# A feed-forward down projection as seven products of quarters

## What is computed

```python
up = rmsnorm(x, g_ffn_pre) @ ffn_w_up
ext = jnp.concatenate([conv_hist, up], axis=1)
c = ffn_conv_b
for j in range(CONV_W):
    c = c + ext[:, j: j + T] * ffn_conv_w[j]
act = jax.nn.gelu(c[..., :D_FF], approximate=True) * c[..., D_FF:]
x = x + rmsnorm(act @ ffn_w_down, g_ffn_post)
```

## Time and profile before

| | us |
|---|---|
| median of 3 runs (lowest to highest) | 1567.13 (1565.37 to 1569.6) |
| the profiled execution, its own time | 1567.42 |
| its span, first to last instruction | 1565.7 |
| TensorE busy | 1524.1 (97%) |
| VectorE busy | 898.4 (57%) |
| ScalarE busy | 583.8 (37%) |
| GpSimd busy | 300.0 (19%) |
| mean granted clock | 0.982 |

### The profile page before, as it was taken

The page is one execution under the profiler, slowest core; times in us unless marked ns, Lnnn a source line. Parts: engine busy times, 40 slices in busy tenths (PEclk is TensorE's granted clock), DMA queues, the critical chain, the costliest instruction groups (busy, mean ns, idle before and its releaser), DMA issues.

```text
span 1565.7 us, 26850 instructions
## 1 busy us (share of the span) xinstructions
PE 1524.1 (97%) x10067; PEld 1415.8 (90%) x10067; DVE 898.4 (57%) x1545; ACT 583.8 (37%) x1084; POOL 300.0 (19%) x293
## 2 busy tenths in 40 slices
PE   7999999999999999999997999999999999999997
PEld 7889999989999999997877999999999998788875
DVE  6575465657332233226558777777777775554644
ACT  7233132333222122114445444444444444453432
POOL 1124133340100000000124333333333320000000
PEclk9999999999999899999998999999999999999999
DMA  7234455451332432304114666655662138665471
GB/s 259 59 109 132 142 174 173 141 173 35 112 113 69 121 110 67 121 14 135 71 45 125 218 218 199 219 191 188 220 221 83 64 111 300 226 216 177 157 243 66
DMA packets 145809, 227.65 MB, mean 145 GB/s; under 512 B 14011, under 2 KB 116441, under 8 KB 144831
## 3 DMA queue, kind: packets, MB, share of 16 engines
q1 hardware_dynamic: 136711, 203.97, 40.8%
q0 software_dynamic: 8736, 22.08, 3.8%
q10 hardware_dynamic: 288, 0.59, 0.1%
HBM read 196.46 MB, written 74.34 MB: 173 GB/s over the span
## 4 chain that ended last, share of the span: by engine, by line
PE 91%; DVE 4%; DMA 2%; ACT 1%; issue 1%; SPq 0%; ACTq 0%; DVEq 0%
PE PS L1323 28%; PE PS L1144 19%; PE PS L1389 13%; PE PS L1039 9%; PE PS L1282 6%; PE PS L1020 4%; PE PS L1208 2%; PE PS L1096 2%; PE PS L1068 1%; PE PS L1384 1%; PE PS L1082 1%; PE PS L1252 1%; PE PS L1001 1%; DMA as_stage<-acts 1%; PE PS L1052 1%
## 5 line engine op out<-in xcount | busy, mean ns | idle before, releaser
L1323 PE MATMUL PS<-h_lo,wr_hi 128*128 128x264 f32 x1056 | 216.7, 286 | 0.0
L1323 PEld LDWEIGHTS PS<-h_lo,wr_hi 128*128 128x128 f32 x1056 | 165.6, 190 | 0.0
L1323 PE MATMUL PS<-t_hi,wr_hi 128*128 128x264 f32 x704 | 149.9, 292 | 7.6 <-DVE h_lo L2296 4.1
L2334 DVE TENSOR_TENSOR wd_lo<-wd_stage,wd_hi 128x1024 fp32r<-128x1024 f32 x66 | 80.8, 1224 | 118.3 <-ACT as_hi L1762 118.2
L1323 PE MATMUL PS<-h_hi,wr_hi 128*128 128x264 f32 x704 | 145.5, 288 | 0.7 <-DVE cext L2362 0.5
L1323 PE MATMUL PS<-t_hi,wr_lo 128*128 128x264 f32 x704 | 145.3, 286 | 0.0
L2020 DVE TENSOR_TENSOR tw_lo<-tw_stage,tw_hi 128x1024 fp32r<-128x1024 f32 (+1 forms) x28 | 32.6, 1166 | 177.7 <-ACT tw_hi L1533 177.5
L1323 PEld LDWEIGHTS PS<-t_hi,wr_hi 128*128 128x128 f32 x704 | 110.8, 191 | 9.1 <-DVE h_lo L2296 4.7
L1761 ACT ACTIVATE wd_hi<-wd_stage 128x1024 fp32r<-128x1024 f32 x66 | 69.8, 1057 | 130.9 <-PE PS L1389 76.6
L1144 PE MATMUL PS<-hT_hi,tw_hi 128*128 128x352 f32 x480 | 111.2, 342 | 1.8 <-issue 1.8
L1323 PEld LDWEIGHTS PS<-h_hi,wr_hi 128*128 128x128 f32 x704 | 108.9, 189 | 3.5 <-DVE wr_lo L2286 0.7
(11 more groups left out here) (317 smaller groups left out, 3444.3 us busy)
## 6 DMA issues: line engine op xcount, KB each, us to landing
wd_stage<-in_ffn_w_down SPq DMA_DIRECT2D x66, 512.0 KB, 3.6
tw_stage<-in_ffn_w_up SPq DMA_DIRECT2D x88, 256.0 KB, 4.8
out_k_s<-in_cache_k_w SPq DMA_DIRECT2D x8, 2044.0 KB
out_v_s<-in_cache_v_w SPq DMA_DIRECT2D x8, 2044.0 KB
qb<-zs SPq DMA_DIRECT2D x24, 512.0 KB, 5.1
acts<-cact POOLq DMA_DIRECT2D x22, 528.0 KB, 9.4
tw_stage<-in_w_in SPq DMA_DIRECT2D x20, 512.0 KB, 5.3
as_stage<-acts SPq DMA_DIRECT2D x44, 192.0 KB, 3.9
```

Of the source, the lines that this page charges most:

```text
L1323: last = pe.matmul(PS[:, bank + b, 0:BH], w[slot][:, k, :], x[:, k, b * BH:(b + 1) * BH], start=(k == 0 and j == 0), stop=(k == HK - 1 and ...
L2334: dve.tensor_tensor(wd_lo[slot][:, :], wd_stage[slot][:, :], wd_hi[slot][:, :].bitcast(F32), ALU.subtract)
```

## The change

The prompt rows of the down projection are cut in two halves of rows, the depth in two halves of 11 blocks, the columns in two halves of 512, and the product of the 2 x 2 quarters is made from seven products in place of eight. A product `n` has 11 steps `(n, k)`, each with 4 row tiles x 3 matmuls of 512 columns; its four tiles lie in four of six PSUM banks, one bank a tile. The three matmuls of a tile are consecutive.

The weights are loaded once in products 1 and 2 and kept (`dw`, 22 blocks of 1024 columns). One quarter of the activations is kept too (`dS`). The other quarters are loaded when needed into four staging buffers (`ds`). GpSimd makes the sums of quarters that Strassen's method needs, 110 operations of 128x512 named in `SUMS` (T1, T4a, T2, T3, T4b on weights; S1, S2, S3, Sa, Sb on activations), each waiting for the one before; they overwrite kept or staged data. Every step is split anew by ScalarE and VectorE, two copies and two subtractions of 128x512, into a ring of three buffers (`ring`); the last four steps of product 3 have buffers of their own. VectorE evicts the products and adds them into two arrays `C1` and `C2` (`evict`), ScalarE copies product 1.

The sample rows (`smp_d`) run apart, against the weights as they are split: the first 512 columns beside products 1 and 2 in bank 6, the second 512 columns as extra steps `(0, k)` in bank 7, each with a split of its own, between the steps of products 6 and 7.

The finishing (squares, gain, reciprocal, multiply and add, store) of the sample tile and of tiles 4 to 6 now lies among the steps of product 3, with the multiplication by the gain on GpSimd for three tiles (`scale_rows`); rows of x come in two buffers (`xrow`), the load of each after the store of the tile two before. Tile 7 and tiles 0 to 3 follow. The split of the fourth step stands behind the copy of the turned tails in ScalarE's order, and on SP the loads from `(1, 6)` on stand behind the wait for the stored convolution states.

The diff, cut to what the text speaks of (the lines taken away are the functions shown above):

```diff
--- before.py
+++ after.py
...
+        HK2, LATE = FC // 2, 4
+        PRODUCTS = (1, 2, 6, 7, 4, 5, 3)
+        SLOTS = []
+        for n in PRODUCTS:
+            for k in range(HK2):
+                SLOTS.append((n, k))
+                if n == 6 and k % 2 and k < 10:
+                    SLOTS.append((0, k // 2))
+                if n == 7 and k % 2 == 0:
+                    SLOTS.append((0, 5 + k // 2))
...
+        SUMS = [("T1", k) for k in range(HK2)] + [(c, k) for k in range(HK2) for c in ("S1", "T4a")]
+        SUMS += [(c, k) for k in range(HK2) for c in ("S2", "T2")] + [(c, k) for k in range(HK2) for c in ("S3", "T3")]
+        SUMS += [("T4b", k) for k in range(HK2)] + [("Sa", k) for k in range(HK2)] + [("Sb", k) for k in range(HK2)]
...
+            def load_down(x):
+                n, k = x
+                u = STAGE[x]
+                st, signal = ds[u % 4], wd_in[u % 4]
+                if u >= 4:
+                    m, l = STAGED[u - 4]
+                    sp.wait_ge(wd_lo_done, AT[STAGED[u - 4]] + 1)
+                    if m in (2, 3, 5):
+                        sp.wait_ge(d_sum, summed_at({2: "S1", 3: "Sb", 5: "Sa"}[m], l))
+                f = k + (HK2 if n in (2, 4, 3) else 0)
...
+            load_down((1, 4))
+            load_s(0)
+            load_down((1, 5))
+            sp.wait_ge(cnat_out, 32 * FC)
+            load_down((1, 6))
+            load_s(1)
+            load_down((1, 7))
+            sp.wait_ge(c_out, 7 * FC + U0)
+            load_s(2)
+            for i in range(2):
+                sp.wait_ge(act_out[i], 16 * (FC // 2))
+            load_smp(1)
+            load_down((1, 8))
...
+            def load_row(i):
+                n = FINAL[i]
+                t0, rows = tile_of(n)
+                if i >= 2:
+                    sp.wait_ge(y_ready, i - 1)
+                else:
+                    sp.wait_ge(wd_lo_done, AT[5, 1 + i] + 1)
+                sp.dma_start(xrow[i % 2][0:rows, :], x2s[t0:t0 + rows, :]).then_inc(wq_in[1][i % 2], 16)
...
+            for x in STAGED[9:]:
+                load_down(x)
+                if x == (3, 5):
+                    load_row(0)
+                    load_row(1)
+            for i in range(NTILE):
+                store_y(i)
+                if i + 2 < NTILE:
+                    load_row(i + 2)
 
...
+            def down_sum(c, k, out, a, b, op):
+                if SUMS.index((c, k)):
+                    pool.wait_ge(d_sum, summed_at(c, k) - 1)
+                pool.tensor_tensor(out, a, b, op).then_inc(d_sum, 1)
...
+            for k in range(HK2):
+                pool.wait_ge(wd_lo_done, AT[1, k] + 1)
+                down_sum("T1", k, dw[k][:, low], dw[k][:, high], dw[k][:, low], ALU.subtract)
+            for k in range(HK2):
+                st = staged(2, k)
+                pool.wait_ge(x_in[k // 4], 16 * (4 if k < 4 else 3))
+                down_sum("S1", k, dS[:, k, :], dS[:, k, :], st[:, 1, :], ALU.add)
+                pool.wait_ge(wd_lo_done, AT[2, k] + 1)
+                down_sum("T4a", k, dw[HK2 + k][:, low], dw[HK2 + k][:, low], dw[k][:, low], ALU.add)
+            for k in range(HK2):
+                st = staged(6, k)
+                down_sum("S2", k, st[:, 0, :], dS[:, k, :], st[:, 0, :], ALU.subtract)
+                down_sum("T2", k, st[:, 1, :], dw[HK2 + k][:, high], dw[k][:, low], ALU.subtract)
+            for k in range(HK2):
+                st = staged(7, k)
+                down_sum("S3", k, st[:, 0, :], st[:, 0, :], st[:, 1, :], ALU.subtract)
+                down_sum("T3", k, st[:, 1, :], dw[HK2 + k][:, high], dw[k][:, high], ALU.subtract)
+            for k in range(HK2):
+                down_sum("T4b", k, dw[HK2 + k][:, low], dw[HK2 + k][:, high], dw[HK2 + k][:, low], ALU.subtract)
+            for k in range(HK2):
+                st = staged(5, k)
+                pool.wait_ge(wd_lo_done, AT[5, k] + 1)
+                down_sum("Sa", k, dS[:, k, :], dS[:, k, :], st[:, 0, :], ALU.subtract)
+
+            def scale_rows(i):
+
+                rows = finished(FINAL[i])
+                pool.wait_ge(o_ss, 9 + i + 1)
+                pool.tensor_tensor(rows, rows, in_halves(gfin[:, :]), ALU.mult).then_inc(t_sums, 1)
+            for k in range(HK2):
+                st = staged(3, k)
+                down_sum("Sb", k, dS[:, k, :], st[:, 0, :], dS[:, k, :], ALU.subtract)
+                if k == 6:
+                    pool.wait_ge(gain_in, 64)
+                    scale_rows(1)
+                elif k == 8:
+                    scale_rows(2)
+            scale_rows(3)
...
+            def tile_part(x, i):
+                n, k = x
+                r, bank = ring(x), (4 * PRODUCTS.index(n) + i) % 6
+                for j, (a, w) in enumerate(((da_hi, dw_hi), (da_hi, dw_lo), (da_lo, dw_hi))):
+                    mm = pe.matmul(PS[:, bank, :], a[r][:, i * P:(i + 1) * P], w[r][:, :],
+                                   start=(k == 0 and j == 0), stop=(k == HK2 - 1 and j == 2))
+                return mm
...
+                if n == 1 and k == 2:
+                    turn_tails(FC - 1)
+            for i in range(4):
+                for x in SLOTS[-LATE:]:
+                    pe.wait_ge(wd_lo_done, AT[x] + 1)
+                    mm = tile_part(x, i)
+                    if i == 3:
+                        mm.then_inc(wd_used, 1)
+                if i < 3:
+                    mm.then_inc(f_mm, 1)
...
+            def split_down(x):
+                n, k = x
+                r = ring(x)
+                if n in (1, 2, 4):
+                    act.wait_ge(wd_in[STAGE[x] % 4], stage_in[x])
+                for c in {4: ("T4b",), 5: ("S1", "T1"), 7: ("T3",), 6: ("T2",), 3: ("Sb",)}.get(n, ()):
+                    act.wait_ge(d_sum, summed_at(c, k))
...
+                    act.wait_ge(p_done, 7 * FC - 3 + U0)
+                if r >= 3:
+                    act.wait_ge(wd_lo_done, AT[5, HK2 - 1] + 1)
+                elif AT[x] >= 3:
+                    act.wait_ge(wd_used, AT[x] - 2)
+                w, a = operands(x)
+                act.activation(dw_hi[r][:, :], w, ACT.Copy)
+                act.activation(da_hi[r][:, :], a, ACT.Copy).then_inc(wd_hi_done, 1)
...
+            for s_, x in enumerate(SLOTS[3:], 3):
+                split_down(x)
...
+                if x == (2, 1):
+                    act.wait_ge(act_out[1], 16 * (FC // 2))
+                    act.wait_ge(wd_used, AT[1, HK2 - 1] + 1)
+                    for i in range(4):
+                        act.activation(C1[:, i, 512:D], PS[:, i, :], ACT.Copy).then_inc(u_out, 1)
+                if x[0] == 3 and 3 <= x[1] < 8:
+                    square(x[1] - 3)
...
+            def evict(n, i):
...
+                p = PRODUCTS.index(n)
+                bank = PS[:, (4 * p + i) % 6, :]
+                left, right = C1[:, i, 0:512], C1[:, i, 512:D]
+                if i < 3:
+                    dve.wait_ge(f_mm, 3 * (p - 1) + i + 1)
+                else:
+                    dve.wait_ge(wd_used, AT[n, HK2 - 1] + 1)
+                if FREED.index((n, i)):
+                    dve.wait_ge(f_free, FREED.index((n, i)))
...
+            dve.wait_ge(cnat_done, FC)
+            for x in SLOTS[3:]:
+                low_down(x)
+                n, k = x
...
+                    if n == 4:
...
+                    for i in range(4):
+                        evict(PRODUCTS[PRODUCTS.index(n) - 1], i)
+                if x == (4, 7):
+                    fold()
+                if n == 3 and k >= 5 and k < 9:
+                    finish(k - 5)
...
```

More of the change, by code:

```diff
@@ L818, in _ @@
-            for n in range(6, NTILE):
-                store_y(n)
+                dst = ys if n == 8 else yp[n * P:n * P + P]
+                sp.dma_start(in_halves(dst), finished(n)).then_inc(y_out[i % 3], 16)
+            for x in STAGED[9:]:
[7 more added lines that the diff above has]
+                    load_row(i + 2)
@@ new lines, in tile_part, with sample_part @@
+            def tile_part(x, i):
[5 more added lines that the diff above has]
+                return mm
+            def sample_part(bank, f, w_hi_, w_lo_, first, last):
+                passes = ((2 * TS, w_hi_), (TS, w_lo_))
+                for j, (both, w) in enumerate(passes[::-1] if last else passes):
+                    mm = pe.matmul(PS[0:both, bank, :], smp_d[f // HK2][:, f % HK2, 0:both], w[:, :],
+                                   start=(first and j == 0), stop=(last and j == 1))
+                return mm
@@ L1852, in _ @@
+            for i in range(5, NTILE):
+                square(i)
         @block.vector
@@ new lines, in fold, with scale_rows @@
+            def fold():
+                dve.wait_ge(wd_lo_done, AT[4, 5] + 1)
+                both = PS[0:2 * TS, 6:8, :]
+                dve.tensor_copy(finished(8), both[TS:2 * TS, :, :]).then_inc(t_step, 1)
+                dve.wait_ge(t_step, U0 + 11)
```

(28 more changed lines are left out.)

346 lines of the change are left out of this document (180 added, 166 removed).

## The result

The changed kernel takes 1608.15 us (median of 4 runs, 1603.6 to 1613.9), the kernel before beside it 1567.4: a ratio of 1.0262, 95% interval 1.0226 to 1.0297. The forecast was 1585 with a range up to 1603: the side was right, the size (+17.6) less than half of the +41 that came. The profiled execution has 1608.4 around a span of 1606.7, 41.0 more than before.

What follows compares the result with a forecast made beforehand. The prediction took TensorE's matmuls to bound the down projection. Terms -30.0 - 1.1 + 3.4 + 4 + 4.9 + 20 + 1.5 + 14 + 0.9 = +17.6 on 1567.4 gave 1585 us, range 1559 to 1603.

Steps and rivals of the forecast that it cites:

- Matmuls: Down projection: full-row matmuls fall from 1056 to 924, 132 fewer at 0.227 us each, -30.0 us.
- the one bank: Three matmuls in a row add into one PSUM bank where two alternate before; forecast at no price.
- the gap after the tails: Sign in product 1: a TensorE gap of about 3 us after the convolution tails are turned.
- The port: Products 6 and 7: GpSimd sums and VectorE subtractions take turns; at least +14, +26.6 by step count, +20 us taken.
- Product 3: Evictions, finishes, GpSimd's wide product and a row load delay the last four steps; +19.5 by step count, +14 us taken.
- Product 1: Start of product 1: fourth step's split waits behind gelu and tails copy, +3.4 us; late loads for steps 7 and 8, +4.
- The heap on SP: Product 1: 5.7 MB of loads come together after the stored convolution states, 13.7 us at 416 GB/s; +4 us, bounds 0 and 6.
- Wait ahead of (6,0): After product 2, GpSimd's late sums delay the first split of product 6: +4.9 us (3.5 to 6.5).
- Head of product 4: Evictions of product 7 stand behind the split of (4,1): +1.5 us (0 to 2.5).
- Tail: Behind the last matmul, an eviction then two finishes take 6.8 us where it was 5.9: +0.9 us.
- -1.1: Down projection before the change: TensorE's one gap of 1.11 us falls away with the 4.2 MB load of x.
- The rival with the clock: TensorE's idle time in products 6, 7 and 3 lowers the granted clock; 1600 us or a little more, chance 0.13.

Runs made afterwards that it cites:

- the first experiment: Changed kernel, with subtractions from split (6,2) to the end of product 7 taking PSUM as second operand: 1587.95 us, ratio 1.0126 to the kernel before.

## Why the prediction fell short, point by point

**Matmuls.** Right: steps of 2.72 and 3.19 wherever nothing is late (product 2 is dense for 35.10), so no price for the one bank. Of the signs that were named, the gap after the tails (about 3, measured 2.90) came; sums of 1.51 (1.7), a TensorE busy for 81% of products 6 and 7 (75 to 80) and 9.1 us of gaps ahead of the last four steps (10 or more) came nearly.

**The port.** The mechanism was right, shown by the first experiment; the size was not. I had followed it step by step with strict turns to +26.6, had a floor of +14, and took the middle, +20. Measured: +30.8. Taking the middle is the step that failed. The rows behind it had turns in them wherever the two kinds of operation met and no case of their missing each other, so nothing spoke for the half towards the floor. The floor itself left out the sums for product 4, which run in this stretch: GpSimd made 51 sums there (x51 in the table beside the added matmuls) and VectorE 66 subtractions, two for each of 33 steps. By an estimate from the earlier trace rows that is 51 x 1.28 + 66 x 0.45 = 95 us of one port; counted in the two timelines, one or the other engine was at such an operation for 95.8 of the 101.0. The rest is in places that I had costed apart or at nothing: an eviction stands behind a split that is late itself (4.58 at the head of product 7).

**Product 3.** The step count said +19.5 (its terms add up to 19.2), I took +14 as between it and 0; measured 49.2 - 29.9 = +19.3. The same error. The count had the cause right: wide products on GpSimd, finishes in front of splits, a late row of x (one finish waited 4.29). That it fits to the tenth is luck: by an estimate 1.9 us of the 19.3 are the slow matmuls behind the last wait, which it didn't have.

**Product 1.** +3.4 and +4 forecast, +11.0 measured. The wait ahead of (1,3) came as 2.90. For it I had named two things in front of the split, the gelu and the copy behind it; the copy is worth 0.3, the gelu and VectorE's product are the wait. The gelu began 10.1 us after the first matmul, 1.2 sooner than before and not 2.5. The heap on SP was there, but two parts of the step were wrong. From 1312.70 to 1328.00 DMA moved 337 GB/s, not 416; and I had not seen the split of the sample rows, which waits for its place in the heap ahead of (1,7). So (1,7) began 9.2 us late, where the forecast had 7.4 for the whole product. The other 1.7 are the four steps behind it at the lower clock, which stood at nothing.

**The rest.** Wait ahead of (6,0): +4.9 forecast, 5.04 measured. Head of product 4: +1.5, measured 1.8. Tail: +0.9, measured 1.8. At nothing stood a wait of 1.10 ahead of (3,0), by which the stretch of product 5 is 1.3 too long, and a start of the stage that is 1.65 later. With -30.0 and -1.1 the measured terms give -31.1 + 1.65 + 11.0 + 5.0 + 30.8 + 1.8 + 1.3 + 19.3 + 1.8 = +41.5, against a span that grew by 41.0.

**The rival with the clock.** It had 1600 or a little more, and the time came out there, with a clock that fell as it said (0.89 in product 6). Still it is not the main reason: in products 6 and 7 the length stayed with the clock brought back. Its price shows only in the lengths of products 1 and 3, behind their last waits: 1.6 us, and by the estimate above 1.9. A time that fits a rival doesn't prove its mechanism. The range ended at 1603 because I gave that case only its beginning; with both step counts in place of the middles the sum would have been 1585 + 6.6 + 5.5 = 1597.

**Open.** 25.4 of the 30.8 us in products 6 and 7 go with their sums and seven of those for product 4; how much the seven hold, and how the other 5 divide between evictions and splits, wasn't taken apart. Nor was the load of the sample rows from the rest of the heap, nor the price of the lower clock in product 3.

## What to carry to other kernels

Before work is put on an idle engine, look whether it shares a path with the engine that feeds the bound one: here GpSimd's sums and VectorE's subtractions of two SBUF tiles make one queue, and their times add up: in strict turns a sum and a subtraction took about 1.7 together. Giving most of both to VectorE, in an order of its own, made products 6 and 7 23 us shorter than sharing. When a step-by-step count rests on rows and the lower bound on hope, take the count. Read a low clock between waits for other engines first as a sign of them: in products 6 and 7 it cost nothing of its own, and over four steps without a wait it cost 1.6 us.

## What the runs showed of the hardware

Where the second operand of a 128x512 subtraction moved from SBUF to PSUM, it went from 1.41 to 0.68 us beside a busy GpSimd, and the sums from 1.57 to 1.29. A wider operation was waited out as well: beside a 128x1024 product on GpSimd (2.42 alone) a 0.68 subtraction lasted 2.86. In products 6 and 7 the granted clock was 0.98 with 63 added matmuls between the steps and 20 ahead of them, 0.92 without, and their length 101.04 both times; the same 56 matmuls with no wait among them took 12.87 us at 1.00 and 14.48 at 0.88.
